# Projecting the unrotated queries of two attention branches with features on partitions, in a two-layer encoder step on one Trainium2 core

## What is computed

```python
qkv_sb, qkv_fox, f_logit, qkv_dsa, q_idx, k_idx, w_idx, gate_logit = jnp.split(h @ w_in, offs, axis=-1)
q_sb, k_sb, v_sb = (a.reshape(b, t, H_SB, HEAD_DIM) for a in jnp.split(qkv_sb, 3, axis=-1))
q_fox, k_fox, v_fox = (...)          # the same, 6 heads of 64
q_dsa, k_dsa, v_dsa = (...)
log_f = jax.nn.log_sigmoid(f_logit + b_forget)
q_dsa, k_dsa = rotary(q_dsa, pos), rotary(k_dsa, pos)   # SB and FOX are not rotated
...
o_sb = stick_breaking_attention(q_sb, ks_sb, vs_sb, pos, k_pos)
o_fox = forgetting_attention(q_fox, ks_fox, vs_fox, g_all[:, -t:], g_all, pos, k_pos)
o_dsa = dsa_attention(q_dsa, ks_dsa, vs_dsa, q_idx, w_idx, ks_idx, pos, k_pos)
```

## Time and profile before

| | |
|---|---|
| median of 3 runs | 2328.32 us (2327.23 to 2329.82) |
| the profiled execution | 2327.93 us |
| its span in the profile | 2325.9 us |
| TensorE busy, share of the span | 2298.8 us, 99% |
| VectorE / ScalarE / GpSimd busy | 1228.4 / 545.2 / 71.0 us |
| bytes moved by DMA | 390.09 MB, mean 168 GB/s |
| the chain that ended last, share on TensorE | 93% |
| layer 0: units 0 to 6 of the projection | 414.7 to 529.5 us |
| layer 0: the 18 groups of transposes | 530.1 to 537.2 us |

### The profile page before, as it was taken

The page is one execution under the profiler, slowest core; times in us unless marked ns, Lnnn a source line. Parts: engine busy times, 40 slices in busy tenths (PEclk is TensorE's granted clock), DMA queues, the critical chain, the costliest instruction groups (busy, mean ns, idle before and its releaser), DMA issues.

```text
span 2325.9 us, 41206 instructions
## 1 busy us (share of the span) xinstructions
PE 2298.8 (99%) x16943; PEld 2050.5 (88%) x16943; DVE 1228.4 (53%) x2671; ACT 545.2 (23%) x1321; POOL 71.0 (3%) x116
## 2 busy tenths in 40 slices
PE   8999999999999999999999999999999999999999
PEld 6999997886688699999999999978856886999999
DVE  4666442633646446666275664426345654666743
ACT  2000022113564231001130001321235642401011
POOL 0000000000022000000000000000000220000000
PEclk9999999999999999999999999999999999999999
DMA  9454334782489353443435533438725984233232
GB/s 338 166 176 157 100 127 150 224 279 90 144 293 346 131 194 110 145 146 100 136 126 177 176 131 121 168 123 248 257 73 178 332 304 149 73 109 109 100 123 77
DMA packets 300466, 390.09 MB, mean 168 GB/s; under 512 B 31078, under 2 KB 250972, under 8 KB 300280
## 3 DMA queue, kind: packets, MB, share of 16 engines
q1 hardware_dynamic: 281688, 337.82, 43.2%
q0 software_dynamic: 11840, 42.30, 5.2%
q10 hardware_dynamic: 6752, 7.33, 0.9%
HBM read 375.30 MB, written 12.12 MB: 167 GB/s over the span
## 4 chain that ended last, share of the span: by engine, by line
PE 93%; DMA 2%; SPq 2%; ACT 1%; DVE 1%; issue 1%; ACTq 0%; DVEq 0%
PE PS L774 31%; PE PS L870 13%; PE PS L1054 6%; PE PS L1322 4%; PE PS L951 4%; PE PS L1002 4%; PE PS L714 3%; PE PS L1140 3%; PE PS L1221 3%; PE PS L918 2%; PE PS L1024 2%; PE PS L926 2%; PE PS L1354 2%; PE PS L1362 2%; DMA BIG<-w_ada 2%; PE PS L1261 2%
## 5 line engine op out<-in xcount | busy, mean ns | idle before, releaser
L774 PE MATMUL PS<-OT,RING 128*128 128x192 f32 x1280 | 234.1, 326 | 0.0
L774 PE MATMUL PS<-H,RING 128*128 128x192 f32 x1280 | 222.1, 327 | 0.0
L774 PE MATMUL PS<-OT,QR 128*128 128x192 f32 x1280 | 221.1, 326 | 0.0
L774 PEld LDWEIGHTS PS<-OT,RING 128*128 128x128 f32 x1280 | 212.4, 190 | 0.0
L774 PEld LDWEIGHTS PS<-H,RING 128*128 128x128 f32 x1280 | 208.4, 190 | 3.8 <-issue 3.2
L774 PEld LDWEIGHTS PS<-OT,QR 128*128 128x128 f32 x1280 | 210.2, 190 | 0.0
L1476 ACT ACTIVATE QR<-QR 128x384 f32<-128x384 f32 x80 | 41.8, 522 | 533.9 <-DVE QR L2075 533.9
L1054 PE MATMUL PS<-H,RING 128*128 128x384 f32 x480 | 161.1, 490 | 0.0
L1054 PEld LDWEIGHTS PS<-H,RING 128*128 128x128 f32 x480 | 88.9, 190 | 60.1 <-issue 3.7
L774 PE MATMUL PS<-H,QR 128*128 128x192 f32 x640 | 117.1, 326 | 0.0
L1931 DVE TENSOR_TENSOR OT<-OT 128x192 f32<-128x192 f32 x154 | 52.8, 353 | 103.7 <-ACT OT L1447 93.6
(11 more groups left out here) (340 smaller groups left out, 3999.9 us busy)
## 6 DMA issues: line engine op xcount, KB each, us to landing
RING<-ffn_w_in SPq DMA_DIRECT2D x80, 1024.0 KB, 7.2
RING<-w_in SPq DMA_DIRECT2D x64, 768.0 KB, 6.4
QR<-w_ada SPq DMA_DIRECT2D x34, 1024.0 KB, 9.9
BIG<-w_ada SPq DMA_DIRECT2D x34, 1024.0 KB, 10.3
RING<-ffn_w_out SPq DMA_DIRECT2D x32, 768.0 KB, 4.6
RING<-ffn_w_out SPq DMA_DIRECT2D x32, 640.0 KB, 5.4
QR<-cache_sb_v POOLq DMA_DIRECT2D x16, 768.0 KB, 5.3
QKT<-cache_sb_k SPq DMA_DIRECT2D x16, 768.0 KB, 6.0
```

Of the source, the lines that this page charges most:

```text
L774: mm = pe.matmul(PS[:, bank, GROUP[g]], a[:, k, :], x[:, k, :], start=(k == 0), stop=(k == 3))
```

## The change

The q columns of SB and FOX are no longer two of the 384-column slabs. Three slabs take their place, one for each pair of heads a: the 128 q columns of pair a of SB beside the 128 q columns of pair a of FOX (256 columns, 1 MB, two transfers with rows of 512 bytes). Each is a unit of seven products over all 384 tokens, with weights as the stationary side and H as the moving one (28 matmuls of 192 columns, no sample part), and its result has features on partitions. These units run first (`u` = 0 to 2); then come five units of the old kind (`u` = 3 to 7) for DSA v, SB k, SB v, FOX k, FOX v. There are eight units and eleven slabs in place of seven and ten; the six `ada_unit`s still follow units 0 to 5.

- VectorE: `half_sums` makes sums of the halves of H once (four additions of 128 x 768), `pair_sums(u)` the weight sums of a pair (four of 128 x 512, one in place in the ring slot). `query_sums` moves behind the sums of unit 2, and `projected_sums(3)` behind `assembled(2)`. `projected_sums` signals after its second and after its fourth addition. Rotation moves to units 3 to 5, the forget scans from unit 4 to unit 6.
- SyncE: the store of the scans moves to slab 10; a load of `w_ada` still goes with slabs 4 to 9.
- ScalarE: the stores move: DSA v to unit 3, SB k and v to unit 5, DSA k, indexer keys and FOX k to unit 6.
- Transposes: six steps of two groups (DSA q and k; then FOX k and SB k) in place of nine, 12 groups in place of 18. The first step no longer waits for the last unit's copies. ScalarE copies the turned DSA q and FOX k, and then the queries of SB and FOX from `QR` to `QKT` and `QBLK`.

```diff
-N_IN, N_OUT, N_PROJ, N_GATE, N_BRANCH, N_WOUT = 11, 8, 10, 8, 4, 2
+N_IN, N_OUT, N_PROJ, N_GATE, N_BRANCH, N_WOUT = 11, 8, 11, 8, 4, 2
...
-PROJ = [6, 7, 9, 8, 0, 1, 2, 3, 4, 5]
-PLAIN_PROJ = 3
-SEVEN_PROJ = N_PROJ - PLAIN_PROJ
+PROJ = [6, 7, 9]
+PLAIN_PROJ = len(PROJ)
+TOKEN_PROJ = [8, 1, 2, 4, 5]
+QPAIRS, TOKENS = NPAIR, len(TOKEN_PROJ)
+SEVEN_PROJ = QPAIRS + TOKENS
+TURNS = 2 * TT
+Q_TAKEN = TURNS + 1
+assert N_PROJ == PLAIN_PROJ + SEVEN_PROJ
...
-                    kind = PROJ[i]
-                    if kind < 9:
+                    kind = (PROJ + [None] * QPAIRS + TOKEN_PROJ)[i]
+                    if kind is None:
+                        d, a = ring(l, r, KD, 2 * P), i - PLAIN_PROJ
+                        load(l, r, [(d[:, :, z * P:(z + 1) * P], w[:, :, COL_QKV[z] + a * P:COL_QKV[z] + (a + 1) * P]) for z in (SB, FOX)])
+                    elif kind < 9:
...
-                    elif i >= 4:
+                    elif 4 <= i < 10:
...
-                    product(0, 0, H[:, lo, 0:P], w[:, lo, GROUP[0]])
-                    product(0, 1, H[:, hi, 0:P], w[:, hi, GROUP[0]]).then_inc(pp_ready, 1)
...
+                    if u < QPAIRS:
+                        w, sw = ring(l, R_PROJ + PLAIN_PROJ + u, KD, 2 * P), SWP[u % 2]
+                        product(0, 0, w[:, lo, 0:P], H[:, lo, GROUP[0]])
+                        product(0, 1, w[:, hi, 0:P], H[:, hi, GROUP[0]]).then_inc(pp_ready, 1)
+                        if pending is not None:
+                            ada_turned(pending)
+                            pending = None
+                        pe.wait_ge(sh_ready, 2 * l + 1)
+                        pe.wait_ge(tp_ready, 2 * g + 2)
+                        if g:
+                            pe.wait_ge(pp_taken, 4 * g)
+                        product(3, 0, sw[:, 1], THP[:, 1]).then_inc(pp_ready, 1)
+                        product(1, 0, sw[:, 0], THP[:, 0])
+                        product(1, 1, w[:, lo, P:2 * P], THP[:, 2]).then_inc(pp_ready, 2)
+                        product(2, 0, sw[:, 2], H[:, hi, GROUP[1]])
+                        product(2, 1, w[:, hi, P:2 * P], THP[:, 3]).then_inc(p2_ready, 1)
+                    else:
+                        w, tp = ring(l, R_PROJ + PLAIN_PROJ + u, KD, MIX), TP[u % 2]
...
+                        pe.wait_ge(sh_ready, 2 * l + 2)
+                        pe.wait_ge(tp_ready, 2 * g + 1)
                         pe.wait_ge(pp_taken, 4 * g)
-                    product(1, 0, SH[0], tp[:, 0])
-                    product(1, 1, SH[2], tp[:, 2]).then_inc(pp_ready, 1)
-                    product(3, 0, SH[1], tp[:, 1]).then_inc(pp_ready, 1)
-                    product(2, 0, SH[3], w[:, hi, GROUP[1]])
-                    product(2, 1, H[:, hi, P:2 * P], tp[:, 3]).then_inc(pp_ready, 1)
-                    if g:
-                        pe.wait_ge(p2_taken, g)
-                    for k in range(KD):
-                        mm = pe.matmul(PS[:, 4, 0:MIX], H[:, k, 2 * P:T], w[:, k, :], start=(k == 0), stop=(k == KD - 1))
-                    mm.then_inc(p2_ready, 1)
+                        product(1, 0, SH[0], tp[:, 2])
+                        product(3, 0, SH[1], tp[:, 3]).then_inc(pp_ready, 1)
+                        pe.wait_ge(tp_ready, 2 * g + 2)
+                        product(1, 1, SH[2], tp[:, 0]).then_inc(pp_ready, 1)
+                        product(2, 0, SH[3], w[:, hi, GROUP[1]])
+                        product(2, 1, H[:, hi, P:2 * P], tp[:, 1]).then_inc(pp_ready, 1)
+                        taken = l * TOKENS + u - QPAIRS
+                        if taken:
+                            pe.wait_ge(p2_taken, taken)
+                        for k in range(KD):
+                            mm = pe.matmul(PS[:, 4, 0:MIX], H[:, k, 2 * P:T], w[:, k, :], start=(k == 0), stop=(k == KD - 1))
+                        mm.then_inc(p2_ready, 1)
...
+                for i in range(TURNS):
+                    tt = i % TT
+                    if i == 1:
+                        pe.wait_ge(pp_taken, 4 * SEVEN_PROJ * (l + 1) - 2)
+                        pe.wait_ge(p2_taken, TOKENS * (l + 1))
+                    if i > 1:
+                        pe.wait_ge(q_taken, l * Q_TAKEN + i - 1)
+                    for a in range(NPAIR):
+                        src = QK[:, DSA, tt, a * P:(a + 1) * P] if i < TT else QK[:, FOX, tt, MIX + a * P:MIX + (a + 1) * P]
+                        mm = pe.transpose(PS[:, turn_bank(i), a * P:(a + 1) * P], src, IDENT[:, :])
+                    mm.then_inc(q_turned, 1)
+                    if i > 1:
+                        pe.wait_ge(k_taken, l * TURNS + i - 1)
+                    for a in range(NPAIR):
+                        mm = pe.transpose(PS[:, turn_bank(i) + 1, a * P:(a + 1) * P],
+                                          QK[:, DSA if i < TT else SB, tt, MIX + a * P:MIX + (a + 1) * P], IDENT[:, :])
+                    mm.then_inc(k_turned, 1)
...
                     if u == 0:
...
-                        store("dsa_v", DSA, VT)
                     if u == 1:
...
                     if u == 3:
+                        store("dsa_v", DSA, VT)
+                    if u == 5:
                         store("sb_k", SB, QK)
                         store("sb_v", SB, VT)
-                    if u == 5:
+                    if u == 6:
                         act.wait_ge(rope_done, l + 1)
...
+                for r in (SB, FOX):
+                    src = qr(r * TT * 2 * MIX, TT * 2 * MIX).rearrange("p (a c) -> p a c", a=NPAIR)
+                    link(A(QKT[:, r, 0, :, :], src[:, :, 0:NPROMPT], ACT.Copy))
+                    ins = sample_queries(r, src[:, :, NPROMPT:T])
+                    if r == SB:
+                        link(ins)
+                ins.then_inc(q_taken, 1)
...
+                def half_sums():
+
+                    for g in range(2):
+                        dve.wait_ge(h_ready[g], 8 * (3 * l + 2))
+                    b11, b12, b21, b22 = (H[:, 4 * i:4 * i + 4, GROUP[g]] for i in range(2) for g in range(2))
+                    begin()
+                    V.tensor_tensor(THP[:, 0], b12, b11, ALU.subtract).then_inc(vch, 1)
+                    V.tensor_tensor(THP[:, 2], b22, b12, ALU.subtract).then_inc(vch, 1)
+                    dve.wait_ge(vch, 1)
+                    V.tensor_tensor(THP[:, 1], b22, THP[:, 0], ALU.subtract).then_inc(vch, 1)
+                    dve.wait_ge(vch, 3)
+                    V.tensor_tensor(THP[:, 3], b21, THP[:, 1], ALU.subtract).then_inc(sh_ready, 1)
+
+                def pair_sums(u):
+
+                    n = l * RINGS + R_PROJ + PLAIN_PROJ + u
+                    dve.wait_ge(slot_full[n % 2], 32 * (n // 2 + 1))
+                    if u > 1:
+                        dve.wait_ge(p2_ready, l * SEVEN_PROJ + u - 1)
+                    w, sw = ring(l, R_PROJ + PLAIN_PROJ + u, KD, 2 * P), SWP[u % 2]
+                    a11, a12, a21, a22 = (w[:, 4 * i:4 * i + 4, z * P:(z + 1) * P] for z in range(2) for i in range(2))
+                    begin()
+                    V.tensor_tensor(sw[:, 0], a21, a22, ALU.add).then_inc(vch, 1)
+                    V.tensor_tensor(a21, a11, a21, ALU.subtract).then_inc(vch, 1)
+                    dve.wait_ge(vch, 1)
+                    V.tensor_tensor(sw[:, 1], sw[:, 0], a11, ALU.subtract).then_inc(vch, 1)
+                    dve.wait_ge(vch, 3)
+                    V.tensor_tensor(sw[:, 2], a12, sw[:, 1], ALU.subtract).then_inc(tp_ready, 2)
...
+                    V.tensor_tensor(tp[:, 3], b22, tp[:, 2], ALU.subtract).then_inc(tp_ready, 1)
+                    if u == QPAIRS:
+                        dve.wait_ge(p2_ready, g)
+                    V.tensor_tensor(tp[:, 0], b22, b12, ALU.subtract).then_inc(vch, 1)
+                    dve.wait_ge(vch, 2)
+                    dve.wait_ge(tp_ready, 2 * g + 1)
+                    V.tensor_tensor(tp[:, 1], b21, tp[:, 3], ALU.subtract).then_inc(tp_ready, 1)
...
+                    r, part = divmod(TOKEN_PROJ[u - QPAIRS] if u >= QPAIRS else 0, 3)
+                    if u < QPAIRS:
+                        base, step = u * 2 * MIX, TT * 2 * MIX
...
-                    dve.wait_ge(pp_ready, 4 * g + 3)
+                    dve.wait_ge(pp_ready, 4 * g + (2 if u < QPAIRS else 3))
                     V.tensor_tensor(U2P, PS[:, 3, GROUP[0]], P1P, ALU.add).then_inc(pp_taken, 1)
                     dve.wait_ge(pp_taken, 4 * g + 2)
+                    if u < QPAIRS:
+                        dve.wait_ge(pp_ready, 4 * g + 4)
...
-                query_sums()
                 dve.wait_ge(gate_ready, l * 24 + 3)
-                projected_sums(0)
+                half_sums()
+                pair_sums(0)
...
-                    if u + 1 < SEVEN_PROJ:
+                    if u + 1 < QPAIRS:
+                        pair_sums(u + 1)
+                    elif u + 1 < SEVEN_PROJ:
+                        if u + 1 == QPAIRS:
+                            query_sums()
+                        else:
```

(73 more changed lines are left out.)

73 lines of the change are left out of this document (29 added, 44 removed).

## The result

The changed kernel takes 2345.18 us (median of 4 runs, 2343.31 to 2347.03) against 2328.41 for the kernel before (4 runs, 2327.23 to 2329.82) beside it: a ratio of 1.0075 with a 95% interval of [1.0062, 1.0087], or +16.8 us. The forecast was 2335.3 with a range of 2325 to 2344. The direction and the central mechanism (a wait behind unit 1) were right; the rise is more than twice the one forecast, 7.0 us, and the median lies 1.2 us outside the range.

A forecast was written before the change was run, and what follows sets the result against it. TensorE, busy 99% of the span, was taken as the bound. Per layer -4.9 saved, +0.5, +6.0, +0.3 of waits and +1.6 of clock gave +3.5; two layers on 2327.93, plus 0.4 for the median, gave 2335.3 us, range 2325 to 2344.

The forecast's parts named there:

- Matmuls, and the 0.63 us ahead of the transposes: TensorE's units: matmuls fall by 1.3 us a layer, and the 0.63 us wait before the transposes goes.
- Unit 1: Behind unit 1, TensorE waits 6.6 us for its `w_ada` block, 0.6 of it there before: +6.0 us a layer.
- the 442.3: Landing time of unit 1's `w_ada` block: 446.3 before, less 4.0 for smaller slabs and a moved store.
- Units 0 and 2: Waits for the `w_ada` blocks behind these pair units: 0.5 us (0 to 1) and 0.3 us (0 to 2).
- The clock: TensorE's clock falls after the idle wait behind unit 1: 1.6 us a layer (0 to 3.2).
- Transposes: Twelve groups at about 0.33 us and one wait take 4.2 us; with the 0.63 us wait gone, 3.6 saved.
- The failed step: Scans' 1.6 MB store ahead of the first gate slab: costed at nothing; 1 to 3 us if cover goes.
- The sum: Per layer -4.9 + 0.5 + 6.0 + 0.3 + 1.6 = +3.5 us; two layers +7.0.
- Much slower: Unit 1's block comes at 446.3 as before, small packets setting the pace: +7.5 us a layer, 2343.3 us; chance 0.14.
- Rival 1: Unit 1's block lands at 440.5, clock stays up: -0.4 us a layer, no change, 2327.5 us; chance 0.23.

The follow-up runs named there:

- blocks_spread: Also 8: changed kernel with cache loads later, scans and their store early, `ada_unit`s behind units 0 and 3 to 7 instead of 0 to 5; 2325.62 us.
- 2: Also caches_late: changed kernel with the forget cache loaded behind slab 6 and indexer keys behind slab 8, both from behind slab 4; 2332.82 us.
- 4: The kernel before with only the forget cache load moved behind slab 6 and the indexer keys behind slab 8; 2327.51 us.
- 5: Changed kernel with 26 extra matmuls on constants, results unused, ahead of TensorE's wait for the `w_ada` block behind unit 1; 2345.99 us.
- 9: Changed kernel with the 26 extra matmuls ahead of the wait behind unit 1, and the scans and their store early; 2335.04 us.
- scans_early: Also 1: changed kernel with the forget scans back behind unit 4 and their store back behind slab 9; 2338.78 us.
- 1 and 2 together: Changed kernel with the scans and their store early and both cache loads behind slabs 6 and 8; 2329.72 us.
- 7: The kernel before with the forget scans behind unit 5 instead of unit 4, so their store is as late as in the changed kernel; 2328.45 us.
- gate_slab_first: Changed kernel with the scans' store issued behind the first gate slab instead of ahead of it; 2343.26 us.
- 10: blocks_spread with the scans' store issued from GpSimd's queue instead of SyncE's; 2329.45 us.

## Why the prediction was right in kind and too small

- **Matmuls, and the 0.63 us ahead of the transposes: right.** Without waits and clock the units take 113.0 us in blocks_spread (115.76 - 2.79; 116.12 - 0.96 - 2.13) and 112.7 in the changed kernel, against 114.7 and 114.6 before (115.43 - 0.57 - 0.17 and 115.32 - 0.68, the three waits of the earlier trace rows): 1.6 to 2.0 us less, forecast 1.9.
- **Unit 1: right in place, cause and size.** TensorE wanted the block at 434.96 (forecast 435.7), had it at 441.28 (442.3) and waited 6.32 and 6.68 us (6.6). SyncE came to it at 430.64 (430 to 432). Experiments 2 and 4 show the cause: the cache loads ahead of it, under a unit too short for them. The terms behind the 442.3 were not all right: pair slabs move slower than I took them (last section), so part of the agreement in size is luck.
- **Units 0 and 2.** 0.60 and 1.72 us (forecast 0.5), and none (0.3). The longer one in layer 1 is 1.2 us of the miss.
- **The clock: right.** 1.55 and 1.65 us against 1.6, and 5 and 9 show it from the other side. The same wait in layer 0 of scans_early cost 2.5 us.
- **Transposes: undersized.** With the store out of the way they take 5.46 us, not 4.2: a saving of 1.7, not 2.9. The pace of 0.33 us held, but I counted one wait of 0.26, and there is also one of 0.78 for ScalarE, which issues FOX v's two stores first; small gaps for its and VectorE's copies are the rest.
- **The failed step: "3.1 MB and 1.2 MB of stores in 19 us, which fit at 227 GB/s. Its cover gone, it would cost 1 to 3 us."** The rate was about right (230 GB/s). But I took the whole stretch as one sum of bytes and did not ask when each transfer would land. The slab is issued 0.7 us behind a store of 15.2 us, and its second transfer takes 20.8 us: it is there 1.65 and 2.43 us too late, in layer 1 with a slower clock behind it (1.7 us). Nor did I see that ScalarE has to issue its own stores in the same time, and stands still when they don't go out. Undoing this move alone gave 6.4 us back, the largest part of the 9.8 by which the rise exceeds the forecast. The trace of before had the store's landing time, 17.1 us, among the DMA issues from 495 us, and I had used only its size:

```profile
scr_g_sample<-QR SPq DMA_DIRECT2D x1, 1584.0 KB, 17.1
```
- **The sum.** Forecast +3.5 a layer. Measured, layer 0: -2.2 (0.2 of it the wait of 0.17 that is gone) + 0.6 + 5.75 + 1.55 + 1.2 (turns) = +6.9; layer 1: -2.0 + 1.7 + 6.0 + 1.65 + 1.4 + 1.7 = +10.5. Less the 2.0 of the earlier starts these are the 15.4 between the profiled executions. The medians lie 16.8 apart, since the profiled run of the changed kernel was the fastest of its four. The units' stage of layer 0 ended at 534.7, not at 536 to 537, since it also started 1.2 us earlier.
- **Not in the prediction at all:** that a late gate slab cancels gains and losses ahead of it (5).
- **The rivals.** Much slower came nearest in size (2343.3), by another mechanism than it named: the block did not come at 446.3. Rival 1's sum leaves out the 0.5 us for unit 0, which would make it 2328.5; that changes nothing here.

Open: 8 still has waits of 5.9 us for `w_ada` and 1.8 for ScalarE, but no run took them away, so a gain from that isn't shown. It isn't shown either why 1 and 2 together are worth 3.3 us less than their sum. Nor is it shown why unit 0 of layer 0 starts now at 413.4, now at 414.8, and in 7 at 418.8.

## What to carry to other kernels

A shorter step on the engine that sets the pace is also a shorter cover: before splitting work, list which transfers are issued under each step and when each has to land, and move these together with the work. When a store moves, take its landing time from the trace (of a load in several transfers the last one's, not the median), and ask for every transfer issued behind it, and every engine that issues one beside it, when that is needed. A gain ahead of a late transfer shows up only as a longer wait, so find the wait that ends the stage last before you judge an edit.

## What the runs showed of the hardware

- Small stores can hold the engine that issues them. Just behind the 1.6 MB store (48 partitions, rows of 2112 bytes), issuing a 64 KB store held ScalarE 4.57 us; with the store early (scans_early) the same issue takes 0.52, and with the store issued about when ScalarE's are (gate_slab_first) 0.66.
- That store was 13.4 to 19.2 us from issue to landing in both layers of all twelve traces, from two queues and at several places in the stage; the longest two are those of gate_slab_first, with a slab issued ahead of it. A block of 2.1 MB takes 6.2 us alone in the queue. Whether the store's 48 partitions or its repeated source set this was not tried.
- The slab of a pair has rows of 512 bytes. The packets of the changed kernel from 432 to 434 us are almost all of them slab 5's:

```profile
DMA packets 1203, 0.61 MB, mean 304 GB/s; under 512 B 17, under 2 KB 1202, under 8 KB 1203
```

At that rate 1.05 MB take 3.4 us, not the 2.3 to 2.6 that I took. The Trainium skill, DMA: Bandwidth & Descriptors, section Specifications, has 512 bytes as the least for full rate; here they reach 304 GB/s, and 336 in another stretch (400 to 402 us), where the rows of `w_ada` reach 403. The measurement decides.
- A wait of 6.3 to 7.6 us on TensorE cost 1.5 to 2.5 us at the lower clock in all six places of after, scans_early and gate_slab_first, and unneeded products in its place saved this. Shorter waits differ: 2.43 us ahead of a gate tile cost 1.7 us, 2.93 us in caches_late 1.5, and 2.79 us in blocks_spread nothing (1.96 us for the `ada_unit` behind it, clock 1.00).
- A transfer can be delayed by one issued after it: the block of 10 by the store in another queue (13.2 us to landing against 9.7).
